# Ranking twelve experts by load on the chip and giving the four lightest one shared set of 32 places

## The reference

```python
y = jnp.zeros_like(t)
for e in range(N_EXPERTS):
    h = jax.nn.silu(t @ w1[e]) * (t @ w3[e])
    y = y + combine[:, e:e + 1] * (h @ w2[e])
```

## Time and profile before

| | us |
|---|---|
| device time, three runs | 635.28, 635.93, 636.02; median 635.93 |
| span of the profiled execution | 634.3 |
| what lies around the span, taken as the median less the span | 1.6 |
| PE busy, share of the span | 620.9, 98% |
| DVE, ACT, POOL busy | 180.1, 139.3, 53.3 |
| bytes moved by the DMA engines | 229.94 MB, mean 362 GB/s |

### The profile page before, as it was taken

How to read it: one execution, slowest core, us unless ns; L and a number is a source line. 1 busy time by engine, 2 the same in 40 slices (tenths; PEclk the granted TensorE clock), 3 DMA queues, 4 the chain that set the end, 5 groups by cost and what they waited for, 6 DMA issues and landing times.

```text
span 634.3 us, 10484 instructions
## 1 busy us (share of the span) xinstructions
PE 620.9 (98%) x4409; PEld 255.9 (40%) x4409; DVE 180.1 (28%) x609; ACT 139.3 (22%) x372; POOL 53.3 (8%) x61
## 2 busy tenths in 40 slices
PE   8999999999999999999999999999999999999996
PEld 5445544434324334333244454453343343343221
DVE  1665834412102102100133667343111021021011
ACT  2136642210000000000131677331100000000011
POOL 0005420000000000000010475000000000000000
PEclk9999999999999999999999999999999999999999
DMA  8999909699999999999999997697999999999993
GB/s 318 293 270 421 385 3 368 228 418 420 422 421 420 422 422 419 421 420 420 399 295 243 346 405 272 239 380 268 421 419 421 421 421 421 421 420 421 419 418 122
DMA packets 44759, 229.94 MB, mean 362 GB/s; under 512 B 8271, under 2 KB 8561, under 8 KB 21666
## 3 DMA queue, kind: packets, MB, share of 16 engines
q1 hardware_dynamic: 43068, 224.66, 90.7%
q0 software_dynamic: 1312, 4.23, 2.0%
q10 hardware_dynamic: 326, 0.31, 0.2%
HBM read 228.10 MB, written 1.08 MB: 361 GB/s over the span
## 4 chain that ended last, share of the span: by engine, by line
PE 91%; DVE 3%; ACT 2%; DMA 2%; issue 1%; POOL 0%; DVEq 0%; ACTq 0%
PE ps L1462 35%; PE ps L1474 18%; PE ps L1220 12%; PE ps L1307 8%; PE ps L1400 5%; PE ps L1431 3%; PE ps L1289 2%; PE ps L1255 2%; PE ps L1276 1%; ACT attw L572 1%; PE ps L1538 1%; PE ps L1444 1%; DMA ring<-bias_rows 1%; DMA x_sb<-in_x_dram 1%; DVE attw L872 1%
## 5 line engine op out<-in xcount | busy, mean ns | idle before, releaser
L1462 PE MATMUL ps<-attw,work 128*32 128x512 f32 x1216 | 140.1, 593 | 0.0
L1474 PE MATMUL ps<-ring,work 128*32 128x512 f32 x960 | 105.0, 593 | 0.5 <-ACT work L651 0.5
L1462 PE MATMUL ps<-ring,work 128*32 128x512 f32 x832 | 100.5, 594 | 0.0
L1220 PE MATMUL ps<-attw,work 128*128 128x512 f32 x192 | 87.4, 598 | 0.1
L1462 PEld LDWEIGHTS ps<-attw,work 128*32 128x32 f32 x1216 | 40.1, 110 | 89.1 <-issue 89.1
L1307 PE MATMUL ps<-attw,work 128*128 128x512 f32 x128 | 60.0, 602 | 0.7 <-issue 0.5
L1474 PEld LDWEIGHTS ps<-ring,work 128*32 128x32 f32 x960 | 30.3, 110 | 70.0 <-issue 68.3
L1025 DVE TENSOR_TENSOR work<-work,ps 128x256 f32<-128x256 f32 (+1 forms) x24 | 11.5, 508 | 156.0 <-PE ps L1462 156.0
L1462 PEld LDWEIGHTS ps<-ring,work 128*32 128x32 f32 x832 | 27.3, 110 | 57.6 <-issue 52.7
L1220 PEld LDWEIGHTS ps<-attw,work 128*128 128x128 f32 x192 | 34.6, 190 | 37.9 <-issue 36.9
L440 POOL TENSOR_SCALAR attw<-attw,stat 128x256 f32<-128x256 f32 x40 | 40.8, 1024 | 51.8 <-DVE stat L886 51.6
(11 more groups left out here) (161 smaller groups left out, 459.9 us busy)
## 6 DMA issues: line engine op xcount, KB each, us to landing
ring<-in_w_dram SPq DMA_DIRECT2D x112, 1024.0 KB, 26.2
attw<-in_w_dram SPq DMA_DIRECT2D x80, 1024.0 KB, 20.2
attw<-in_w_qkv_dram SPq DMA_DIRECT2D x4, 2048.0 KB, 17.4
attw<-in_w_o_dram SPq DMA_DIRECT2D x8, 1024.0 KB, 22.9
attw<-in_w_qkv_dram SPq DMA_DIRECT2D x8, 512.0 KB, 11.0
ring<-bias_rows POOLq DMA_DIRECT2D x16, 256.0 KB, 7.2
x_sb<-in_x_dram SPq DMA_DIRECT2D x2, 512.0 KB, 7.0
out_dram<-x_sb SPq DMA_DIRECT2D x2, 512.0 KB, 4.5
```

What stands on the lines that cost most here:

```text
L1220: last = pe.matmul(ps[:, g, :], xT[:, k, P * tt:P * tt + P], wqkv[part][:, k, :], start=(k == 0), stop=(k == KB - 1))
L1462: last = pe.matmul(ps[row:row + SLOTS, bank[t], :], xg[:, k, t, row:row + SLOTS], w[:, e, k % 4, :], start=(k == 0), stop=(k == KB - 1), t ...
L1474: last = pe.matmul(ps[row:row + SLOTS, bank[t], :], hT[t][:, k, row:row + SLOTS], w[:, e, k % 2, 512 * half:512 * half + 512], start=(k == ...
```

## The change

The second group (`POOLED = 1`) no longer holds experts 4 to 7, but the four of experts 4 to 15 with the fewest tokens in both tiles together. Each of them has 32 places for both tiles, instead of 32 for each; groups 2 and 3 hold the other eight, in order of rank, and group 0 still holds experts 0 to 3. The counts are taken earlier, ahead of the ranking matmul of tile 1; DVE makes the order (`copy_counts`, `order_experts`), the places and the weights by rank (`rank_places`, `rank_weights`), SP reads the expert numbers into registers and forms the source addresses of units 12 to 47 from them. The transfers keep their sizes, but for the half units (12 and 47), which become two transfers of 0.5 MB each where there was one of 1 MB. In the pooled group a unit pair is used together. If one of the four has more than 32 tokens in all, the flag is raised. The further rounds keep the old order.

```diff
+        def pooled_down_unit(p, kh):
+            return UPS + 2 * kh + p
+        def first_rank(g):
+            return 0 if g == POOLED else PER_GROUP * (g if g < POOLED else g - 1)
+        def is_pooled(m, g):
+            return m is main and g == POOLED
...
+            def ranked_source(L, n, e, experts):
+                g, j = divmod(n, UNITS)
+                if j < UPS:
+                    which, kh, p = j // 4, j // 2 % 2, j % 2
+                    of = ranked_up[which]
+                else:
+                    kh, p = divmod(j - UPS, 2) if g == POOLED else divmod(j - UPS, 2)[::-1]
+                    of = ranked_down
+                return of[L, bass.ds(experts[2 * p + e], 1), kh].rearrange("o p f -> p (o f)")
+            def load_ranked(L, n, experts):
+                dst = held[n % HELD].rearrange("p (e f) -> p e f", e=2)
+                for e in range(2):
+                    sp.dma_start(dst[:, e], ranked_source(L, n, e, experts)).then_inc(held_landed[n % HELD], 16)
...
+            def experts_at(first, count):
+                return [sp.value_load(order_i[0:1, r:r + 1], min_val=0, max_val=EXPERTS - 1) for r in range(first, first + count)]
...
             def wait_used(L, n):
                 g, j = divmod(n, UNITS)
                 Q = GROUPS * L + g
-                if j < UPS:
+                if g == POOLED:
+                    if j < UPS:
+                        sp.wait_ge(main.w13_used, UPS * Q + 2 * (j // 2) + 2)
+                    else:
+                        sp.wait_ge(main.w2_used, DOWNS * Q + 4 * ((j - UPS) // 2) + 4)
+                elif j < UPS:
                     sp.wait_ge(main.w13_used, UPS * Q + j + 1)
                 else:
                     sp.wait_ge(main.w2_used, DOWNS * Q + 2 * (j - UPS) + 2)
             def load_stream(L):
                 sp.wait_ge(first_half_used, L + 1)
-                for n in (HELD, HELD + 1):
-                    load_half(L, n, 0)
-                for n in (HELD, HELD + 1):
+                load_half(L, HELD, 0)
+                sp.wait_ge(order_ready, L + 1)
+                experts = experts_at(first_rank(1), 2)
+                load_ranked_half(L, HELD + 1, 0, experts)
+                wait_used(L, 0)
+                load_half(L, HELD, 1)
+                experts += experts_at(first_rank(1) + 2, 2)
+                wait_used(L, 1)
+                load_ranked_half(L, HELD + 1, 1, experts)
+                for n in range(HELD + 2, LAST):
+                    if n % UNITS == 0:
+                        experts = experts_at(first_rank(n // UNITS), PER_GROUP)
                     wait_used(L, n - HELD)
-                    load_half(L, n, 1)
-                for n in range(HELD + 2, LAST):
-                    wait_used(L, n - HELD)
-                    load_held(L, n)
+                    load_ranked(L, n, experts)
                 wait_used(L, LAST - HELD)
-                load_half(L, LAST, 0)
-                load_half(L, LAST, 1, last_half_landed)
+                load_ranked_half(L, LAST, 0, experts)
+                load_ranked_half(L, LAST, 1, experts, last_half_landed)
...
+                    if is_pooled(m, g):
+                        h = h_sb[0].rearrange("p (k q) -> p k q", k=FB)
+                        up = ps[:, W[0], :].rearrange("p (q k) -> p k q", k=FB)
+                        for ks in (slice(0, 2), slice(2, FB)):
+                            act.activation(h[:, ks], up[:, ks], ACT.Silu).then_inc(m.silu_done, 1)
+                        for n, ks in enumerate((slice(0, 2), slice(2, FB))):
+                            act.wait_ge(m.ht_done, TURNS * R + TT * g + n + 1)
+                            act.copy(hT[0][:, ks, :].rearrange("p k s -> p (k s)"),
+                                     ps[:, (V[1], W[0])[n], 0:2 * P]).then_inc(m.ht_copied, 1)
+                        act.wait_ge(m.w2_used, DOWNS * Q + 8)
+                        act.copy(y_sb[:, 1, 0, :], ps[:, W[0], :]).then_inc(m.y1_copied, 2)
...
+            def copy_counts(L):
+                dve.wait_ge(counts_done, L + 1)
+                step(dve.tensor_copy(counts, ps[:, 0, 96:96 + TT * E]))
+                step(dve.tensor_tensor(sums, counts[:, PER_GROUP:E], counts[:, E + PER_GROUP:2 * E], ALU.add))
+                step(dve.scalar_tensor_tensor(key, slot_no[:, PER_GROUP:E], 1.0 / E, sums, ALU.mult, ALU.add))
+            def order_experts(L):
+                step(dve.tensor_tensor(by_rank[:, 0], across(key), down_rows(key), ALU.is_lt))
+                step(dve.tensor_reduce(rank_of, by_rank[:, 0], AX, ALU.add))
+                step(dve.tensor_tensor(is_at, across(rank_of), down_rows(slot_no[:, 0:X]), ALU.is_equal))
+                step(dve.tensor_tensor(by_rank[:, 0], is_at, across(slot_no[:, PER_GROUP:E]), ALU.mult))
+                step(dve.tensor_reduce(key, by_rank[:, 0], AX, ALU.add))
+                dve.tensor_copy(order_i, key).then_inc(order_ready, 1)
+                dve.wait_ge(order_ready, L + 1)
+            def rank_places():
+                step(dve.scalar_tensor_tensor(moved, rank_of, float(PER_GROUP), counts[:, PER_GROUP:E], ALU.is_lt, ALU.mult))
+                step(dve.tensor_tensor(moved, moved, sel[:, 1, PER_GROUP:E], ALU.mult))
+                step(dve.tensor_tensor(posm[:, 1, PER_GROUP:E], posm[:, 1, PER_GROUP:E], moved, ALU.add))
+                for t in range(TT):
+                    ins = dve.tensor_tensor(by_rank[:, t], is_at, across(posm[:, t, PER_GROUP:E]), ALU.mult)
+                step(ins)
+                step(dve.tensor_reduce(pos_ranked[:, :, :], by_rank, AX, ALU.add))
+            def rank_weights():
+                for t in range(TT):
+                    ins = dve.tensor_tensor(by_rank[:, t], is_at, across(comb[:, t, PER_GROUP:E]), ALU.mult)
+                step(ins)
+                step(dve.tensor_reduce(comb_ranked[:, :, :], by_rank, AX, ALU.add))
             def see_overflow(L):
-                dve.wait_ge(counts_done, L + 1)
-                step(dve.tensor_reduce(sum_g[:, 0:1], ps[:, up_banks(0)[1][1], 0:TT * E], AX, ALU.max))
+                step(dve.scalar_tensor_tensor(single_sums, rank_of, float(PER_GROUP), sums, ALU.is_lt, ALU.mult))
+                step(dve.tensor_reduce(sum_g[:, 0:1], work[:, 3072:3072 + TT * E + X], AX, ALU.max))
                 dve.tensor_scalar(flag[:, L:L + 1], sum_g[:, 0:1], float(SLOTS), None, ALU.is_gt).then_inc(flag_ready, 1)
                 dve.wait_ge(flag_ready, L + 1)
...
+            def of_group(m, g, tt, of, count, plain, ranked):
+                if m is main and g:
+                    first = first_rank(g) + of
+                    return ranked[:, tt, first:first + count].unsqueeze(2).broadcast_to([P, count, SLOTS])
+                first = PER_GROUP * g + of
+                return plain[:, tt, first:first + count].unsqueeze(2).broadcast_to([P, count, SLOTS])
...
+            def copy_pooled(L, m, Q, n, bank):
+                dve.wait_ge(m.gathered, 2 * TT * Q + n + 1)
+                ks = slice(2 * n, 2 * n + 2)
+                dve.tensor_tensor(xg[:, ks, 0, :], ps[:, bank, 0:2 * P].rearrange("p (k c) -> p k c", k=2),
+                                  next_gains[:, L, ks].unsqueeze(2).broadcast_to([P, 2, P]),
+                                  ALU.mult).then_inc(m.xg_copied[n // 2][n % 2], 1)
...
-                weigh_places(0, g)
-                weigh_places(1, g).then_inc(m.pc_built, 1)
+                weigh_places(m, 0, g)
+                weigh_places(m, 1, g).then_inc(m.pc_built, 1)
                 if m is main and g == 0:
+                    rank_weights()
                     see_overflow(L)
...
                 copy_gathered(L, main, GROUPS * L, 0, 0, 6)
                 choose(L, 1)
                 place(L, 1)
+                copy_counts(L)
                 copy_first_blocks(L)
+                order_experts(L)
+                rank_places()
                 copy_gathered(L, main, GROUPS * L, 1, 0, 6, slice(2, 4))
...
-                def count(bank):
-                    pe.matmul(ps[:, bank, 0:TT * EXPERTS], ones[:, :], rt[7][:, 0:TT * EXPERTS],
+                def count():
+                    pe.wait_ge(sel_ready, TT * (L + 1))
+                    pe.matmul(ps[:, 0, 96:96 + TT * EXPERTS], ones[:, :], rt[7][:, 0:TT * EXPERTS],
                               start=True, stop=True).then_inc(counts_done, 1)
...
+                def gather_pooled(m, n, bank):
+                    for k in range(2):
+                        c = (2 * n + k) * P
+                        for t in range(TT):
+                            last = pe.matmul(ps[:, bank, P * k:P * k + P], x_sb[:, t, c:c + P], pg_flat[:, t, :],
+                                             start=(t == 0), stop=(t == TT - 1))
+                    last.then_inc(m.gathered, 1)
...
+                def pooled_group(m, R, g, built, landed, unit):
+                    Q = GROUPS * R + g
+                    W, V = up_banks(g)
+                    def up_both(which, kh):
```

(50 more changed lines are left out.)

132 lines of the change are left out of this document (90 added, 42 removed).

## The result

Four executions of the changed kernel took 641.97, 642.22, 642.42 and 643.86 us, median 642.32. The kernel before, run beside it, has a median of 635.97 over four. The ratio is 1.0107, 95% interval [1.0093, 1.0121] (the medians alone give 1.0100). So the change costs about 1%, some 6.4 us between the medians; forecast were 636.7 us and a range up to 639.6.

The account below looks back on a forecast made before the run. The prediction took the unbroken weight transfers, not PE, as the bound. Per layer 0.25 + 0.2 - 0.1 = 0.35 us, rounded up to 0.4, two layers 0.8: span 634.3 to 635.1, with 1.6 around it 636.7; range 635.2 to 639.6.

Parts of the forecast that it names:

- The main step: Expert phases: the weight transfers are the limit, so saving 41.8 us of PE gains only 0.1 us a layer.
- Order_experts: Six DVE steps behind copy_first_blocks, 1.9 us: order_ready at 122.4, before first_half_used at 122.8, so covered by 0.4 us.
- Count before rank: Counting ahead of tile 1's ranking matmul delays the chain to the stream's start by 0.25 us a layer (0.15 to 0.35).
- Rank_places: DVE steps of 1.7 us making places by rank; last gathered blocks about 0.9 us late, covered by PE's lead: nothing.
- the reads in later groups: Four SP reads at each later group, 2 to 4 us against a queue of over 20 us: nothing.
- SP's registers: Two SP reads before unit 12's issue, at the stream's start: a hole of 0 to 0.4 us, taken as 0.2.
- the edit that was costed at nothing: Half units sent as two transfers of 0.5 MB instead of one of 1 MB; no cost of their size was forecast.
- The rival of the hole: Stream's start: second issue later than 2.5 us after the first, 0.5 to 2 us a layer, 637.8 to 640.8; chance 0.27.
- the clock: Waiting PE drops to 1.2 GHz; behind unit 43 that costs 2 to 6 us a layer, 640 to 648; chance 0.04.
- What is won at unit 43 is the wait itself: PE's saving gains only its wait for unit 43 near a layer's end, under 0.1 us a layer.

Follow-up runs that it names:

- b_half_pe: The kernel before with half of the blocks k of the second group left out in up and down, nothing else changed: 637.16 us, ratio 1.0026.
- static_tail: The changed kernel with unit 12 fixed in two 1 MB transfers, register reads behind it, and the last group's w3 worked by unit: 634.29 us, ratio 0.9984.
- a_reads: The changed kernel with unit 12 from fixed experts in 1 MB transfers, the order wait and SP's reads left in place: 638.71 us, ratio 1.0049.
- v_big: v_all with unit 12 sent as two transfers of 1 MB instead of four of 0.5 MB: 634.72 us, ratio 0.9991.
- a_tail: The changed kernel with all of unit 42's part of the last group's w3 done before the wait for unit 43: 638.75 us, ratio 1.0041.
- a_awake: The changed kernel with idle matmuls put ahead of PE's waits for unit 43 and unit 30: 640.88 us, ratio 1.0080.
- a_static12: The changed kernel with unit 12 from fixed experts, sent at once in 1 MB transfers, SP's reads of the order behind it: 637.15 us, ratio 1.0030.
- a_small: The changed kernel with unit 12 from fixed experts in four 0.5 MB transfers, no reads ahead of it: 638.75 us, ratio 1.0048.
- bhp_tail: b_half_pe with the last group's w3 order of a_tail, no ranking in it: 634.62 us, ratio 0.9982.
- v_all: The changed kernel with all of unit 11 sent first, unit 12 by register behind it in four 0.5 MB transfers, and a_tail's order: 636.54 us, ratio 1.0015.
- v_all_again: v_all unchanged, run again beside v_big on the same chip: 637.04 us, ratio 1.0016.

## Why the prediction was wrong

**What held.** The main step did: the transfers are the limit, and 41.8 us of PE are worth 0.1 us. b_half_pe, which gains nothing from it, shows it alone, and PE at 93% with the rates unchanged shows it in the changed kernel. PE's idle grew by 16.8 us a layer, forecast were 15 to 20. *Order_experts* ended at 122.61 (122.4 forecast), half a us ahead of the first issue at 123.09, so the wait for `order_ready` cost nothing. A step of 144 columns took 0.30 to 0.31 us, as taken:

```profile
120.75 0.30 DVE L1028 TENSOR_TENSOR work<-work 128x144 f32<-128x144 f32 x1
...
122.44 0.17 DVE L1033 CAST stat<-work 128x12 int32<-128x12 f32 x1
```

*Count before rank*, 0.25 us a layer, fits what can be seen, but is not shown: from the transposes of x to the first issue in layer 1 the ten kernels with the early count took 115.25 to 115.76 us, the four without it 115.02 to 115.50, three of them 115.02 to 115.05; the ranges overlap by the kernel before, with 115.50. *Rank_places* and the reads in later groups cost nothing, by static_tail. PE busy fell by 27.8 us and not 40: at 1.2 GHz the same matmuls count for longer, and the four stretches at half clock hold 5.46 + 2.68 + 5.37 + 3.41 = 16.9 us of busy time, of which half, 8, is the clock's; the last 4 are not accounted for.

**The first failed step: "SP's registers", a hole of 0 to 0.4 us, taken as 0.2.** The issue came where the sum had it, 1.97 us behind the first in a range of 1.5 to 2.9. What was wrong is the cover of 2.49 us, the size of one transfer over the full rate. The stream starts from standing engines; with little queued behind each transfer the rate was 275 to 306 GB/s for several us. In a_reads the second issue comes 1.84 and 1.55 us behind the first, well inside the cover, and still costs about 0.5 us. And the edit that was costed at nothing, two transfers of 0.5 MB for one of 1 MB, has a price of its own: about 0.5 us a layer alone, as much as the reads, and 1.35 together with them by the rates. The term should have read 1.3 to 1.8 us a layer, by the rates and by the heads, in place of 0.2. The rival of the hole had the right size for this (0.5 to 2 us a layer), but its condition, a second issue later than 2.5 us, was not met and did not decide.
The Trainium skill, DMA: Bandwidth & Descriptors, "Latency and other measured facts", gave about 0.6 us for such a load. The rows show 0.27 and 0.48 us here, so the page is over them, and by either figure the issue stays inside the cover: it was not the reads' length that failed. v_big, with the same reads and more queued ahead, loses 0.2 us by the rates and nothing by the heads.

**The second failed step: the clock, a rival with a chance of 0.04.** Its mechanism was named rightly, and also the place where it hurts, "in the 25 us behind unit 43"; its size (2 to 6 us a layer) was too large, for it measured 1.3 and 1.7, and its chance was far too small. Two sentences made it so. "It waits about 1 to 1.5 us per unit" spreads the waiting evenly, but the order of the last group stood in the code: only 16 of unit 42's 32 instructions come before the wait for unit 43, so the waiting gathers into one of 3.06 us. And in "attention has waits of that size at full clock" the size compared was 1.5 us, not 3. a_tail and a_awake, with waits of 1.32 and 0.63 us for unit 43, kept the clock behind it.
The Trainium skill, TensorE: Matmul & The Clock Gate, "HAM oscillation", tells of short bursts between waits for transfers and a fall each time, and advises to order the work so that PE stays busy. The trace agrees on where it falls and with the advice, but not on "each time": b_half_pe's wait of 3.05 us let it fall in one layer and not in the other.

**A term that the sum did not have.** "What is won at unit 43 is the wait itself" holds only for the order as it was. With slack the work behind unit 43 can be cut from 48 matmuls to 32, for 0.7 us a layer. It is small, but it is the one gain that these runs show.

So the loss of 5.9 us is two costs of about 3.0, each of them written down beforehand as a rival and each given too little: 0.36 for slower was the right sign in the rivals and the wrong weight. The range missed the 642.3 since it took in one of the two and never both.

## What to carry to other kernels

Taking work off an engine that a stream of transfers already paces gives nothing, and it turns a steady walk into waits: look in the code for where the waiting will gather, since one wait of 2 to 3 us just ahead of the last, uncovered work can halve the clock for it. A queue that starts from empty needs more behind it than one transfer's time: put large transfers with fixed addresses ahead of anything that must wait for a register, and lay the data out so that computed addresses don't split them. To see what an idea can give at best, run it first with its overheads left out (static_tail).

## What the runs showed of the hardware that was not expected

- The clock fell behind a wait of 3.05 us in one layer and not in the other of the same execution (b_half_pe). In a_reads, behind 3.06 and 3.05 us, and in a_static12, behind 3.05 twice, it fell in neither layer; in the changed kernel and in a_small it fell in both. That makes five falls in ten waits of 3.03 to 3.06 us. Behind the twelve waits of 1.18 to 1.35 us for unit 43 (a_tail, bhp_tail, static_tail, v_all, v_all_again, v_big) it never fell. But it fell once behind a wait of 2.13 us (a_tail, at 597.83) and once behind one of 2.30 us (a_awake, at 578.40), where it cost nothing that shows. The stretches at 1.2 GHz were 3.41, 6.83 and once 10.24 us long.
- Small transfers on a queue that has just started run at a lower rate with busy engines: 315 against 401 GB/s over 5 us, at a share of 0.97 against 1.00 (v_all_again, v_big). "Busy" is there partly single packets that take longer: in the changed kernel's 440.5:445 the packets of 4 KB have a median of 159 ns as in the kernel before, but a mean of 206 and a longest of 1142, where the kernel before, as long after its first issue, has a mean of 159 and a longest of 199. At the end of a full queue four of 0.5 MB cost nothing that shows: v_big's last unit lands 0.1 us off the pace.
  The Trainium skill, DMA: Bandwidth & Descriptors, "Bandwidth", advises transfers of 1 MiB and more, by measurements on GpSimd's queue; on SP's queue here the heads agree with it, the end of the stream does not need it.
- A DMA with its address in a register costs SP little more. The issue itself has a median of 350 ns, where the fixed one at 123.09 has 378; a move of 29 ns and an operation of 42 ns stand beside it, and from one such issue to the next it is 0.53 to 0.55 us where it was 0.42:

```profile
L383 SPq MOVE ring<-in_w_dram x4: 29/29/29, 125.0 to 128.9; - x4
L383 SPq DMA_DIRECT2D ring<-in_w_dram x4: 340/350/512, 125.1 to 129.0; - x4
L383 SPq FUSED_REGOPS  x3: 42/42/47, 125.5 to 128.9; - x3
```

Left open: a count taken behind the ranking matmul, to save its 0.25 us a layer, wasn't tried; pooling a later group, whose order is not wanted at the stream's start, wasn't either.
